# Two expert-layer schedules changed together: looked-up rows in every half step of the selection, later builds, and three more places for dense units

## The reference, cut to what matters

```python
def block(xc):                                  # 128 tokens
    q = (xc @ w_q).reshape(PEER_CHUNK, PEER_HEADS, 2, half)
    sc = jnp.einsum('thpd,hpnd->thpn', q, subkeys).astype(jnp.float32)
    s1, i1 = lax.top_k(sc[:, :, 0], PEER_TOPK)
    s2, i2 = lax.top_k(sc[:, :, 1], PEER_TOPK)
    cand = (s1[..., :, None] + s2[..., None, :]).reshape(PEER_CHUNK, PEER_HEADS, ncand)
    cidx = (i1[..., :, None] * PEER_N_KEYS + i2[..., None, :]).reshape(PEER_CHUNK, PEER_HEADS, ncand)
    top, pos = lax.top_k(cand, PEER_TOPK)
    idx = jnp.take_along_axis(cidx, pos, axis=-1).reshape(PEER_CHUNK, PEER_HEADS * PEER_TOPK)
    gate = jax.nn.softmax(top, axis=-1).reshape(PEER_CHUNK, PEER_HEADS * PEER_TOPK)
    u_e = jnp.take(u, idx, axis=0)
    v_e = jnp.take(v, idx, axis=0)
    act = jax.nn.gelu(jnp.einsum('ted,td->te', u_e, xc).astype(jnp.float32))
    return jnp.einsum('te,ted->td', (gate * act).astype(v_e.dtype), v_e)
```

## Time and profile before

| | |
|---|---|
| timed runs | 2060.38, 2061.05, 2070.07 us |
| profiled execution | 2069.18 us, its span 2067.4 |
| TensorE busy | 97% of the span |
| VectorE | 67% |
| ScalarE, GpSimd | 32%, 28% |
| DMA, mean rate | 296 GB/s |
| layer 0: first sweep, second sweep | from 258, from 573 us |
| layer 1: first sweep, second sweep | from 1073, from 1384 us |

### The profile page before, as it was taken

One profiled execution on the slowest core, in us unless ns is written; L12 is line 12 of the kernel. 1 busy time (PEld: TensorE's weight loads), 2 busy tenths in 40 slices (PEclk: granted clock), 3 DMA queues, 4 the chain that ended last, 5 costly groups with the idle time before them and its releaser, 6 DMA issues.

```text
span 2067.4 us, 33110 instructions
## 1 busy us (share of the span) xinstructions
PE 2003.5 (97%) x13084; PEld 1837.4 (89%) x13084; DVE 1377.5 (67%) x2724; ACT 656.5 (32%) x1331; POOL 579.4 (28%) x539
## 2 busy tenths in 40 slices
PE   9999999999999998989999999999999899999999
PEld 9878899999999887977699999999988898777887
DVE  7567589877755444458849977784535627877885
ACT  4455411344400000036540144430000105765554
POOL 1000103767644333200101386754343410000000
PEclk9999999999999999999999999999999999999999
DMA  7536777999999999914467999999999974334564
GB/s 265 192 133 214 254 246 297 383 409 405 394 402 409 409 409 409 393 62 143 154 246 264 342 410 408 407 399 409 409 406 409 409 298 136 112 124 135 190 192 166
DMA packets 169273, 612.42 MB, mean 296 GB/s; under 512 B 19984, under 2 KB 20096, under 8 KB 168864
## 3 DMA queue, kind: packets, MB, share of 16 engines
q1 hardware_dynamic: 107712, 391.63, 51.3%
q0 software_dynamic: 59984, 217.28, 27.0%
q10 hardware_dynamic: 1424, 1.41, 0.2%
HBM read 606.89 MB, written 1.05 MB: 294 GB/s over the span
## 4 chain that ended last, share of the span: by engine, by line
PE 70%; DMA 17%; DVE 9%; issue 2%; ACT 1%; POOL 1%; ACTq 0%; SPq 0%; POOLq 0%; DVEq 0%
PE ps L1015 21%; PE ps L1046 15%; DMA plain<-in_peer_v 10%; PE ps L719 5%; DMA plain_in_xs<-in_peer_v 5%; PE ps L755 4%; PE ps L758 4%; PE ps L762 4%; PE ps L802 3%; PE ps L722 3%; PE ps L791 2%; PE ps L1002 2%; PE ps L854 1%; DVE big L2384 1%; DMA big<-in_peer_ur,big 1%
## 5 line engine op out<-in xcount | busy, mean ns | idle before, releaser
L1046 PE MATMUL ps<-big,plain 128*128 128x160 f32 x2784 | 406.2, 304 | 22.0 <-DMA plain<-in_peer_v 17.7
L1046 PEld LDWEIGHTS ps<-big,plain 128*128 128x128 f32 x2784 | 384.6, 191 | 41.8 <-issue 23.1
L2557 DVE SCALAR_TENSOR_TENSOR big<-big 128x1024 f32<-128x1024 f32 x166 | 213.3, 1285 | 216.0 <-DMA big<-in_peer_v,big 214.3
L1015 PE MATMUL ps<-big,plain 128*128 128x160 f32 x2160 | 310.4, 302 | 3.1 <-issue 3.1
L2137 DVE TENSOR_TENSOR lo<-raw,hi 128x1024 fp32r<-128x1024 f32 (+1 forms) x195 | 236.1, 1219 | 113.7 <-ACT hi L1530 113.1
L1015 PEld LDWEIGHTS ps<-big,plain 128*128 128x128 f32 x2160 | 298.5, 191 | 4.2 <-issue 4.2
L3239 POOL DMA_INDIRECT big<-in_peer_v,big x168 | 174.3, 1037 | 295.4 <-DVE big L2557 152.8
L1530 ACT ACTIVATE hi<-raw 128x1024 fp32r<-128x1024 f32 (+1 forms) x195 | 204.7, 1055 | 157.0 <-PE ps L762 53.2
L3239 POOL DMA_INDIRECT big<-in_peer_ur,big x132 | 162.5, 1231 | 155.9 <-DVE big L2551 122.2
L1015 PE MATMUL ps<-big,plain_in_xs 128*128 128x160 f32 x1376 | 199.7, 303 | 3.4 <-issue 3.4
L1046 PE MATMUL ps<-big,plain_in_xs 128*128 128x160 f32 x1312 | 192.8, 305 | 10.4 <-DMA plain_in_xs<-in_peer_v 8.0
(11 more groups left out here) (413 smaller groups left out, 2803.9 us busy)
## 6 DMA issues: line engine op xcount, KB each, us to landing
plain<-in_peer_v SPq DMA_DIRECT2D x174, 512.0 KB
plain<-in_peer_u SPq DMA_DIRECT2D x135, 512.0 KB
plain_in_xs<-in_peer_u SPq DMA_DIRECT2D x86, 512.0 KB
plain_in_xs<-in_peer_v SPq DMA_DIRECT2D x82, 512.0 KB
big<-in_peer_u SPq DMA_DIRECT2D x35, 512.0 KB, 7.0
raw<-in_ret_vg SPq DMA_DIRECT2D x32, 512.0 KB, 3.5
raw<-in_peer_q SPq DMA_DIRECT2D x24, 512.0 KB, 4.2
raw<-in_ffn_up SPq DMA_DIRECT2D x22, 512.0 KB, 3.6
```

Source lines behind the costliest of these rows:

```text
L1015: ins = e.matmul(u.view[:, j * DENSE:(j + 1) * DENSE], w[:, k, :], Peer.xT[:, k, :], start=k == 0, stop=k == 7)
L1046: ins = e.matmul(us[b // 2].view[:, b % 2 * DENSE:(b % 2 + 1) * DENSE], w[:, b * 128:(b + 1) * 128], experts[:, k, :], start=k == 0 and b ...
L2557: e.scalar_tensor_tensor(out=sums, in0=rows, scalar=w, in1=sums, op0=ALU.mult, op1=ALU.add).then_inc(s_looked, 1)
```

## The change

Two things. First, a look stands in every half step of pairs 8 to 13 (before, in four of five up to pair 11 and in the first half of pairs 12 and 13); the lists are turned two pairs later, the first build comes at pair 27 instead of 26, and builds then stand in four of seven half steps instead of five of nine. Second, dense units get three more places: one in `lefts`, used as the ring's eleventh, free when the last query halves are added; and two where the looked-up sums are kept later, free when the last key scores are computed and used up to load 127. For these two the selection's scratch `eq` moves from there into tile 0's scores.

```diff
-N_PLAIN, N_FIRST, IN_XS, N_ROWS, IN_RAW, LATE = 20, 6, 4, 9, 3, 6
+N_FIRST, IN_XS, IN_EXPERTS, IN_SUMS, N_ROWS, IN_RAW, LATE = 6, 4, 10, 2, 9, 3, 6
+N_RING = N_FIRST + IN_XS + 1
+N_PLAIN = N_RING + IN_EXPERTS + IN_SUMS
-YIELDS, GATED, TURNED, LISTED, SPREAD, LOOKS = 15, 14, 22, 23, 26, 8
+YIELDS, GATED, TURNED, LISTED, SPREAD, LOOKS = 15, 14, 24, 25, 27, 8
 def unit_slots(l):
-    until = {10 + j: min(49, UNIT * j // (2 * DENSE) * 2 + 1) for j in (range(2, 8) if l else range(10))}
-    last = {**{s: -30 + s for s in until}, **{s: -10 + s for s in range(10)}}
-    until.update({s: 209 if l and s >= N_FIRST else 255 for s in range(10)})
+    until = {N_RING + j: min(49, UNIT * j // (2 * DENSE) * 2 + 1) for j in (range(2, 8) if l else range(IN_EXPERTS))}
+    last = {**{s: -30 + s for s in until}, **{s: -10 + s for s in range(N_RING)}}
+    until.update({s: 209 if l and s >= N_FIRST else 255 for s in range(N_RING)})
+    for s in range(N_RING + IN_EXPERTS, N_PLAIN):
+        until[s], last[s] = 127, 1
...
-            n = 1 if c >= SPREAD and (2 * (c - SPREAD) + j) % 9 % 2 == 0 else 0
+            n = 1 if c >= SPREAD and (2 * (c - SPREAD) + j) % 7 % 2 == 0 else 0
...
-            n = 1 if c >= LOOKS and q < LISTS and ((2 * (c - LOOKS) + j) % 5 < 4 if c < GATED - 2 or c >= SPREAD else j == 0) else 0
+            n = 1 if c >= LOOKS and q < LISTS and (c < GATED or ((2 * (c - LOOKS) + j) % 5 < 4 if c >= SPREAD else j == 0)) else 0
...
+        plain.append(nc.alloc_sbuf_tensor_at("plain_in_lefts", [128, UNIT], F32, offset=lefts_at)[:, :])
+        plain += [big[:, i * UNIT:(i + 1) * UNIT] for i in range(IN_EXPERTS)]
+        plain += [big[:, 128 * DENSE + i * UNIT:128 * DENSE + (i + 1) * UNIT] for i in range(IN_SUMS)]
...
+        def plain_free(l, slot):
+            if slot >= N_RING + IN_EXPERTS:
+                return use["pk", l, 1, 1, 1].filled
+            if slot == N_RING - 1:
+                return s_added, pair_sums(l, 5)
+            return s_used, split_before[l, slot] + 1
...
-            cand, eq = flat[:, 0:896], flat[:, 2048:3072].bitcast(BF16)
+            cand, eq = flat[:, 0:896], sc[:, 0, 0:1024].bitcast(BF16)
```

More of the change, by code:

```diff
@@ L298, in build @@
         plain = [plain_a[:, i, :] for i in range(N_FIRST)] + [plain_b[:, i, :] for i in range(IN_XS)]
-        plain += [big[:, i * UNIT:(i + 1) * UNIT] for i in range(N_PLAIN - len(plain))]
+        plain.append(nc.alloc_sbuf_tensor_at("plain_in_lefts", [128, UNIT], F32, offset=lefts_at)[:, :])
+        plain += [big[:, i * UNIT:(i + 1) * UNIT] for i in range(IN_EXPERTS)]
+        plain += [big[:, 128 * DENSE + i * UNIT:128 * DENSE + (i + 1) * UNIT] for i in range(IN_SUMS)]
         xh, xl = xs[:, :, 0, :], xs[:, :, 1, :]
@@ L667, in build @@
                 split_before[l, i] = max(n for n in in_ring[i % N_SPLIT] if n < end) if i < N_FIRST else \
-                    end - 1 if i < N_FIRST + IN_XS else W.first[f"peer_q{l}"] - 1
+                    end - 1 if i < N_RING else W.first[f"peer_q{l}"] - 1
             for r in range(N_SPLIT):
@@ L3355, in plain_load @@
                 if SLOTS[l][i] not in SLOTS[l][:i]:
-                    e.wait_ge(s_used, split_before[l, SLOTS[l][i]] + 1)
+                    e.wait_ge(*plain_free(l, SLOTS[l][i]))
                 else:
@@ L3367, in sp @@
                     unit_load(n)
-                    if n >= end - 9 and SLOTS[l][early] >= 10:
+                    if n >= end - 9 and SLOTS[l][early] >= N_RING:
                         plain_load(l, early)
```

## The result

The changed kernel is slower, by little. Over 12 runs each it took 2065.0 us (2061.63 to 2073.09), the kernel before 2062.03 us (2058.67 to 2070.07). The ratio is 1.0019, with a 95% interval of 1.0011 to 1.0027: 3.9 us more, where the prediction had 3.0 us less. The profiled execution took 2067.16 us. First its span and its stretches, as the earlier trace rows: us, five engines with busy time and instructions, granted clock, DMA share, GB/s.

The account below looks back on a forecast made before the run. The prediction took TensorE as the chain, its pace set by the DMA in the second sweep. Terms of -6.6 us there and +3.6 us for builds gave -3.0 us, 2058.0 us from a 2061.05 median, range 2046 to 2069.

Parts of the forecast that it names:

- the price of the builds: First sweep: builds later against TensorE, costing 2.1 us in layer 0 and 1.5 in layer 1, +3.6 us together.
- rival 2: Instruction-fetch stalls in the first burst of gathers come or go, some 8 us either way, 2050 or 2066; chance 0.14.
- pair 30, two looks more: TensorE's spreads at pair 30 need builds with two more looks ahead of them, 5.1 us at 2.56 us each.
- what the prediction took (3): First sweep: the row stream runs 3 us earlier, set against the 5.1 us of two more looks.
- I take 3.3 us a layer: Second sweep: one more load in reserve and two gathers fewer save 3.3 us a layer, 6.6 in all.
- that of the gathers: Second sweep: 108 looks and gathers instead of 110, two loads fewer at 1.28 us each of the DMA.
- its low count of 2.1 us: Second-sweep gain if gathers near the end wait for TensorE and the dense stream gets more than half the DMA.
- either of its counts (1.28 or 2.56): Second sweep: one reserve load is worth 1.28 us by plain bytes, 2.56 us if each stream gets half the DMA.
- Rival 1: The stall of the first gather burst goes, covered by more dense places; 8 and 7 us, 2043 us; chance 0.14.
- Rival 3: Rows come ahead by one look only, builds 4 us later, two stops of TensorE; 23 us less 6.6, 2073; chance 0.12.
- Rival 4: Nothing comes through: the lead is used up before the second sweep and the builds are just met; 2061 us; chance 0.12.
- the first starved unit: Second sweep: TensorE's first unit starved of data was to come two to seven units later.

Follow-up runs that it names:

- before_again: The kernel before the change, unchanged, profiled a second time; 2061.3 us (one execution).
- after: The changed kernel with both parts of the change, against the kernel before; 2065.0 us, ratio 1.0019.
- before: The kernel without the change; 2062.03 us over 12 runs.
- sched_only: The kernel before with only the new tables (looks, lists and builds), dense places as before; 2067.5 us, ratio 1.0022 to 1.0046 against the kernel before.
- places_only: The kernel before with only the three more dense places and the scratch moved for them; 2056.8 us, ratio 0.9970 to 0.9988 against the kernel before.
- lefts_only: The kernel before with only the one new place in the lefts; 2059.4 us, ratio 0.9978 to 0.9996 against the kernel before.
- old_later_places: The kernel before with the three new places and the looks of pairs 21 to 25 moved to pairs 29 to 40; 2049.7 us, ratio 0.9925 to 0.9951.
- old_looks_later: The kernel before with only the looks of pairs 21 to 25 moved to pairs 29 to 40; 2057.3 us, ratio 0.9972 to 0.9990.
- looks_later: The changed kernel with the looks of pairs 22 to 26 moved to pairs 30 to 41; 2052.5 us, ratio 0.9944 to 0.9971 against the kernel before.
- sums_only: The kernel before with only the two new places in the sums; 2061.4 us, ratio 0.9992 to 1.0010 against the kernel before.
- the first profile: The profiled execution of the unchanged kernel from which the prediction was read; 2069.18 us.
- three_later: The changed kernel with only the looks of pairs 24 to 26 moved to pairs 30 to 37; 2053.9 us, ratio 0.9950 to 0.9975 against the kernel before.
- before_busy7: The kernel before with the dense matmuls of pairs 20 to 22 issued twice; 2076.2 us, ratio 1.0060 to 1.0086 against the kernel before.

## Why the prediction was wrong

**The sum against the sweeps.** The forecast was -6.6 in the second sweeps and +3.6 in the first. Between before_again and after, two single executions, it is -2.7 and -0.6, together -3.3, and +2.7 and +3.5, together +6.1. So -3.0 became +2.9. Of the miss of 5.9 us, 3.3 lie in the second sweeps and 2.6 in the builds; most of both (2.7 and 2.0) is in layer 1.

**The step that failed in the first sweep** is the price of the builds, where the prediction says "that leaves the builds 2.1 us later against TensorE" and, for layer 1, "a little slack is left at the other steps, and I take 1.5 us". Both rest on when TensorE asks, and that time came from an execution in which it had stopped for 8 and 7 us. The prediction saw these stops, and counted with them only as time that may come or go (rival 2). It did not ask what they hide. With a delay of 8.7 us put in by added work the price is 2.1 and 2.8 us; without it the step is slower by 2.7 and 3.5, and before_again shows that before was already paying 3.94 and 2.65 us in waits.

I also looked at the wrong step. The working counts at pair 30, two looks more. The wait is at the first spread, where four more stand ahead: the first build comes behind look 20 in before and behind look 24 in after. Four looks at 2.56 us are 10.2. Look 24 starts at 392.97 in after and at 395.05 in before_again, 2.1 us earlier; after's sweep began 1.1 later, so counted from there the row stream is 3.1 us ahead, which is what the prediction took (3). That term was right, and the count of looks was not. From the sweep's start the build is 7.1 us later, as the two spreads show (387.09 and 395.21, less the 1.1), and TensorE comes a pair, 4.3 us, later. The rest, 2.7, is the difference of the waits, 6.65 - 3.94. The slower clock behind the wait takes 1.2 us more than in before_again (4.56 for 3.39), about as much as the stop of 1.05 us at 406.93 that only before_again has.

**The second sweep.** The step that failed here is "I take 3.3 us a layer". The three loads fewer were counted about right for layer 0: in that sweep the DMA moves 122.36 MB in after and 123.72 in before_again, 2.6 loads, by 1.28 us 3.3. For layer 1 it is 124.30 and 125.21 MB, 1.7 loads, 2.2 us. The sweeps gave 2.7 and 0.6. The two parts of the change alone (sched_only, places_only) give, in layers 0 and 1, -1.2 and -0.1 us for the tables and -1.2 and -1.4 for the places. By the prediction's count of bytes one place is a load, 1.28 us, and two gathers fewer are 2.56. So the places gave what they were to give, and the term that failed is that of the gathers, 1.3 us in both layers for 5.1. All of these are single executions, and lefts_only (0.5 and 3.2) shows that the split over the layers is not firm. Part of the miss is seen near the sweep's end. The stretch from 270 to 290 us into layer 1's second sweep, of before_again and of after:

```profile
1646.51:1666.51 20.00, 18.96 (x127) 17.14 (x126) 9.25 (x8) 0.00 (x0) 3.75 (x4) 1.00 1.03 408
```

```profile
1652.93:1672.93 20.00, 19.23 (x133) 17.87 (x132) 8.75 (x7) 0.00 (x0) 3.98 (x6) 1.00 0.99 386
```

The last gather goes out 273 us into the sweep in after and 281 in before_again, and the DMA is no longer full behind it. Over the whole sweep its mean rate is 399.05 GB/s for 401.23, by which 1.7 us of the 2.2 saved in bytes are lost. The prediction knew this loss, as its low count of 2.1 us, and took 3.3. The prediction's own remark, that the place in layer 1 ends at load 209, was not made a term of the sum; lefts_only, where layer 1 is the one that gains, speaks against it as the cause. Why layer 1 loses more than layer 0 stays open.

The runs also show when the places pay. Beside moved looks (old_later_places against old_looks_later) they shorten the second sweeps by 3.1 and 2.7 us, more than the prediction gave to a place by either of its counts (1.28 or 2.56); beside the old looks (places_only against before_again) by 1.2 and 1.4. The difference is visible ahead of the second sweep. The stretch 500:570 of before_again, of after, and of looks_later:

```profile
500.00:570.00 70.00, 70.00 (x580) 69.43 (x580) 53.08 (x103) 28.84 (x96) 46.76 (x38) 1.00 1.01 393
```

```profile
500.00:570.00 70.00, 70.00 (x585) 69.39 (x584) 53.00 (x105) 31.64 (x105) 47.23 (x39) 1.00 0.98 371
```

```profile
500.00:570.00 70.00, 70.00 (x576) 69.51 (x575) 56.22 (x107) 26.35 (x88) 43.68 (x35) 1.00 1.03 407
```

In after the DMA runs at 371 GB/s here (365 in 1310:1370 of layer 1), 38 under its full rate: 2.7 MB or five loads not made in this stretch, while TensorE works without a stop. My reading, argued from these rows and not tested alone, is that the places were full. Two more runs fit it: places_only and sums_only, whose first sweeps are about as long as before_again's, have 375 and 381 GB/s in 500:570 for 393; loads made early by more places would be loads not made there. By this reading loads are saved in the second sweep only where the DMA is full up to its start.

**The rivals.** Rival 1 looked right on the page, since the stops of the burst are gone; but they are gone in before_again too, so the change has no part in it. Rival 2, stops that come or go, is what sets the first profile apart from the others, and not the change from the kernel before. Rival 3 had the mechanism: builds late, one stop in one piece, a slow clock behind it. Its condition, rows ahead by one look only, did not hold (3.1 us), and its size was wrong, 23 us for some 6, as no second stop follows in after: look 29 starts at 404.42, 11 us before the point that it named. Rival 4 is refuted in its reason: something came through on both sides.

**What was right:** 12 looks before the gates, the gates 4.4 us later (368.28 for 363.85 in before_again), of which 1.1 is the sweep's later start, so 3.4 as worked out, the new load in SyncE's gap, and the places in the sums worth nothing. Wrong: the first starved unit comes no later (a wait of 1.45 us 155 us into the second sweep of layer 0, of 1.89 us after 158 in before_again), and the sweeps are 2.7 and 0.6 us shorter, not 3 to 4.

## What to carry to other kernels

Before a price is read off a wait, look whether the engine that waits came late in that execution: a stall upstream makes every producer behind it look punctual, and a second profile of the same kernel would have shown it. In an in-order queue, count what stands ahead of the first item that another engine asks for, not of a typical one; work that goes at the DMA's pace (here five looks) belongs behind it. Time won ahead of a DMA-bound stretch can go again in it: of the 12 us that the moved looks won in the first sweeps, 7 went in the second, and with three more places 1.3. Looks moved and places added gave 3.9 and 4.3 us alone, and 12.8 together.

## What the hardware showed

- The stops on "issue" of TensorE and VectorE in the first burst of gathers, 8 and 7 us, were in the first profile (2069.18 us) and in none of the 16 profiles taken since, of this kernel and its variants. What sets them off is open.
- After a wait in one piece TensorE's next unit of 16 records took 3.39 us (wait 3.94), 4.56 (6.65), 3.51 (6.92) and 3.96 (2.60, layer 1 of three_later) instead of 2.34; after the 3.19 us of three_later's layer 0 it took 2.39. So the length of the wait alone doesn't tell the price.
- Added work was paid to the tenth where nothing waited: 8.7 us more gave 311.78 us and 13.0 more gave 316.12 (before_busy7), in both layers, against 303.08, which old_looks_later and old_later_places show in all four of their first sweeps.
